# A one-core decoder step: modulation rows laid out whole, a zero fill and the decode work in other places

## The reference

```
mod = einsum('nd,de->ne', silu(c), ada_w) + ada_b          # 9 rows of 6 x 1024
sh1, sc1, g1, sh2, sc2, g2 = split(mod, 6)
h = rmsnorm(x, norm1_g) * (1 + sc1) + sh1
q, k, v, u = split(h @ w_in)                               # 8 heads of 64; u is 512 wide
att = dilated_attn_prompt(q, k, v, rel_bias)               # prompt rows: causal, three dilations
att = dilated_attn_decode(q, [cache_k, k], [cache_v, v])   # sample rows: over 2048 cached rows each
ssm_y, state = s5_branch(u, ...)                           # scan, GELU, then per-group GLU
mixed = concat(rmsnorm(att), rmsnorm(ssm_y))
x = x + g1 * (mixed @ w_out)
h2 = rmsnorm(x, norm2_g) * (1 + sc2) + sh2
x = x + g2 * hier_moe(h2)                                  # 16 experts, 2 of one group per token
y = rmsnorm(x, final_norm_g)
```

## Time and profile before

| | |
|---|---|
| runs | 800.74, 802.43, 807.8 us; median 802.43 |
| profiled execution | 809.11 us; span of its instructions 807.2 us |
| PE busy | 676.1 us (84%) |
| DVE, ACT, Pool busy | 291.5, 176.4, 126.4 us (36, 22, 16%) |
| mean granted clock of PE | 0.909 |
| DMA | 211.89 MB, mean 263 GB/s |
| chain that ended last | PE 69%, DMA 16%, SP's queue 5%, DVE 5%, ACT 3% |

### The profile page before, as it was taken

How to read it: one execution, slowest core, us unless ns; L and a number is a source line. 1 busy time by engine, 2 the same in 40 slices (tenths; PEclk the granted TensorE clock), 3 DMA queues, 4 the chain that set the end, 5 groups by cost and what they waited for, 6 DMA issues and landing times.

```text
span 807.2 us, 12020 instructions
## 1 busy us (share of the span) xinstructions
PE 676.1 (84%) x4885; PEld 392.6 (49%) x4885; DVE 291.5 (36%) x694; ACT 176.4 (22%) x362; POOL 126.4 (16%) x224
## 2 busy tenths in 40 slices
PE   3669999999999776899999499976899999999800
PEld 2558698888873343434456454422344444333200
DVE  4799665771111343325373641101110111110148
ACT  6010331222224365332121001100110100110033
POOL 2320006657500123110000000000000000000040
PEclk9879899999999988899987579999899999999955
DMA  8996147483784987997114929999999639999562
GB/s 285 386 265 231 58 160 270 161 283 112 226 183 152 365 323 180 364 344 254 59 59 177 319 65 388 395 391 409 396 399 374 234 105 364 396 401 400 218 238 110
DMA packets 93613, 211.89 MB, mean 263 GB/s; under 512 B 8716, under 2 KB 15404, under 8 KB 93269
## 3 DMA queue, kind: packets, MB, share of 16 engines
q1 hardware_dynamic: 82582, 182.49, 63.5%
q0 software_dynamic: 4976, 18.37, 7.3%
q10 hardware_dynamic: 6000, 10.25, 3.4%
HBM read 197.42 MB, written 18.91 MB: 268 GB/s over the span
## 4 chain that ended last, share of the span: by engine, by line
PE 69%; DMA 16%; SPq 5%; DVE 5%; ACT 3%; issue 2%; POOL 1%; ACTq 0%; POOLq 0%; DVEq 0%
PE ps L2555 18%; PE ps L2099 11%; PE ps L2597 9%; PE ps L2415 7%; DMA whalf<-in_w_down 5%; PE ps L2001 4%; DMA ring<-in_cache_v 4%; PE ps L2069 3%; PE ps L2007 2%; DMA ring<-in_ada_w 2%; SPq L510 2%; PE ps L2241 2%; PE ps L2216 1%; DMA whalf<-in_w_up 1%; SPq L660 1%
## 5 line engine op out<-in xcount | busy, mean ns | idle before, releaser
L2555 PE MATMUL ps<-whalf,xgT 128*128 128x512 f32 (+2 forms) x576 | 174.1, 612 | 9.1 <-DMA whalf<-in_w_up 5.2
L2555 PEld LDWEIGHTS ps<-whalf,xgT 128*128 128x128 f32 (+2 forms) x576 | 66.7, 158 | 107.8 <-issue 102.9
L2597 PE MATMUL ps<-whalf,aT 128*128 128x512 f32 (+2 forms) x288 | 87.8, 629 | 12.8 <-DMA whalf<-in_w_down 10.8
L2099 PE MATMUL ps<-hT,ring 128*128 128x272 f32 x384 | 91.4, 394 | 0.0
L2099 PEld LDWEIGHTS ps<-hT,ring 128*128 128x128 f32 x384 | 71.8, 190 | 15.2 <-issue 1.4
L2597 PEld LDWEIGHTS ps<-whalf,aT 128*128 128x128 f32 (+2 forms) x288 | 33.4, 160 | 60.3 <-issue 57.8
L2415 PE MATMUL ps<-ring,mixT 128*128 128x512 f32 x128 | 60.8, 634 | 1.9 <-ACT mixT L837 1.9
L807 POOL DMA_INDIRECT xg<-h_d,gidx x12 | 11.4, 948 | 226.4 <-PE ps L2001 185.3
L2415 PEld LDWEIGHTS ps<-ring,mixT 128*128 128x128 f32 x128 | 25.5, 203 | 32.7 <-issue 30.5
L1889 DVE COPY ysb<-ps 128x512 f32<-128x512 f32 x12 | 8.3, 691 | 91.6 <-PE ps L2597 91.6
L2069 PE MATMUL ps<-hT,ring 128*32 128x136 f32 x1024 | 36.8, 303 | 5.2 <-DVE hT L1373 4.0
(11 more groups left out here) (417 smaller groups left out, 921.0 us busy)
## 6 DMA issues: line engine op xcount, KB each, us to landing
whalf<-in_w_down SPq DMA_DIRECT2D x32, 1024.0 KB, 16.1
whalf<-in_w_gate SPq DMA_DIRECT2D x32, 1024.0 KB, 14.1
whalf<-in_w_up SPq DMA_DIRECT2D x32, 1024.0 KB, 14.3
ada_half<-in_ada_w SPq DMA_DIRECT2D x16, 1024.0 KB, 5.4
ring<-in_cache_k SPq DMA_DIRECT2D x8, 1792.0 KB, 7.7
ring<-in_cache_v SPq DMA_DIRECT2D x6, 2048.0 KB, 11.7
ring<-in_ada_w SPq DMA_DIRECT2D x4, 2048.0 KB, 14.7
ring<-in_w_in SPq DMA_DIRECT2D x4, 2048.0 KB, 13.4
```

What stands on the lines that cost most here:

```text
L2099: ins = mm(ps[:, z % 2, 0:2 * NCOL], r[:, 512 * k + P * (c % 4):512 * k + P * (c % 4 + 1)], hT[:, k, 2 * h:2 * h + 2, :].rearrange("p a b ...
L2555: ins = mm(out[cols, :], xgT[b][:, k, cols], r[:, 512 * (k % 4):512 * (k % 4 + 1)], start=k == 0, stop=k == KD - 1, **tile_at(m_, n))
L2597: ins = mm(ps[cols, 6 + n2, :], aT[:, t % 2, c, cols], r[:, c0:c0 + 512], start=c == 0, stop=c == 3, **tile_at(m_, n))
```

## The change

1. SP stores the modulation a second time, as nine whole rows of 4096 numbers (`mod_r`, nine DRAM-to-DRAM transfers after `kv(1)`). `mod2r`, `mod3P`, `mod3S` and `g2P` are read from there, so a piece is 12, 4 or 0.5 KB. `mod3P` is issued after `kv(12)` instead of `kv(9)`.
2. The zero fill of `y_d` goes from before the attention loop to behind the second store of `h2`, on the same Pool queue.
3. Pool clears `glu2` between two steps of the scan, and builds `qbd` before it fills `glu2`.
4. Group 0's keys stand between the V products, its softmax and transposes around the last one, group 1's keys between the bias tiles. `dPT` lies in another place of SBUF, and the new rows of V pass through another PSUM bank.
5. In the loop only group 1's transposes (round 1) and the values remain: group 0's in rounds 3 to 6, group 1's in rounds 8 to 11.

```diff
     def mod_rows(n, first):
-        return bass.AP(mod_d.tensor, 2 * first * P * P, [[0, P], [P * P, 2 * n], [32 * P, 4], [1, P]])
+        return bass.AP(mod_r.tensor, D * (first - 2), [[0, P], [1, D * n]])
...
             if i == 1:
...
-                for c in range(4):
-                    sp.dma_start(mod2r[4 * c:4 * c + 4, :],
-                                 bass.AP(mod_d.tensor, (6 + c) * P * P, [[32 * P, 4], [1, P]])).then_inc(s("cld"), 16)
-            if i == 9:
+                for r in range(NC):
+                    sp.dma_start(mod_r[r].rearrange("(c j n) -> c j n", j=4, n=P),
+                                 bass.AP(mod_d.tensor, P * (4 * P + r), [[P * P, 8], [32 * P, 4], [1, P]]))\
+                        .then_inc(s("cld"), 16)
+            if i == 3:
+                sp.wait_ge(s("cld"), 16 + 16 * NC)
+                sp.dma_start(mod2r[:, :], mod_r[0, D:3 * D].rearrange("(a n) -> a n", n=P)).then_inc(s("cld"), 16)
+            if i == 12:
                 sp.wait_ge(s("glut"), 16)
...
-                sp.dma_start(mod3P[:, :, :].rearrange("p v (c j n) -> p (v c) j n", c=2, j=4),
-                             mod_rows(3, 2)).then_inc(s("mod3"), 16)
+                sp.dma_start(mod3P[:, :, :].rearrange("p v n -> p (v n)"), mod_rows(3, 2)).then_inc(s("mod3"), 16)
...
         turn_back(4)
+        pool.wait_ge(s("xp"), len(BATCH))
+        o(pool.memset(glu2[:, :, :, :], 0.0))
         turn_back(5)
...
-        pool.dma_start(y_d[NREG * P:NTILE * P, :], I["zero"].partition_broadcast(EXTRA * P)).then_inc(s("yzero"), 16)
...
             pool.dma_start(h2_d[tok(j), :], h2[0:TW[j], p % 2, :]).then_inc(s_h2st[p % 2], 16)
+            if p == 1:
+                pool.dma_start(y_d[NREG * P:NTILE * P, :], I["zero"].partition_broadcast(EXTRA * P)).then_inc(s("yzero"), 16)
...
-        for n in range(16):
-            glu_out(n)
...
+        for n in range(10):
+            glu_out(n)
         dec_softmax(0)
+        dec_probs(0)
+        for n in range(10, 16):
+            glu_out(n)
+        dec_softmax(1)
...
         for n in range(3):
             glu_in(n)
+        dec_keys(0, 0)
         z_two(9)
...
             glu_in(n)
+        dec_keys(0, 2)
+        dec_keys(0, 3)
         z_two(11)
         v_t(2)
+        dec_probs_t(0)
         for n in range(10, 13):
             glu_in(n)
         v_t(3)
+        dec_keys(1, 0)
...
             if st == 1:
-                dec_probs_t(0)
-            if 2 <= st < 6:
-                dec_keys(1, st - 2)
-            if st == 6:
-                pe.wait_ge(s("cld"), 80)
+                dec_probs_t(1)
+                pe.wait_ge(s("cld"), 32 + 16 * NC)
                 tr(ps[:, 7, 0:16], mod2r[:, :]).then_inc(s("pe_prep"), 1)
-            if 9 <= st < 13:
-                if st == 9:
-                    pe.wait_ge(s("dve_prep"), M2E)
-                dec_values(0, st - 9)
-            if st == 13:
-                dec_probs_t(1)
-            if 14 <= st < 18:
-                dec_values(1, st - 14)
+            if st == 3:
+                pe.wait_ge(s("dve_prep"), M2E)
+            if 3 <= st < 7:
+                dec_values(0, st - 3)
+            if 8 <= st < 12:
+                dec_values(1, st - 8)
```

More of the change, by code:

```diff
@@ L203 @@
 GP, MODTP, DBP, M2P, ATTSP = range(1, 6)
-KMZ, PADT, BPAD, GLUB, QBD = range(1, 6)
+KMZ, PADT, BPAD, QBD, GLUB = range(1, 6)
 MODT, HMA, KME, SSRT = 1, 2, 3, 16
@@ L439, in mod_rows @@
     def mod_rows(n, first):
-        return bass.AP(mod_d.tensor, 2 * first * P * P, [[0, P], [P * P, 2 * n], [32 * P, 4], [1, P]])
+        return bass.AP(mod_r.tensor, D * (first - 2), [[0, P], [1, D * n]])
     def mod_rows_seq(n, first):
-        return bass.AP(mod_d.tensor, P + 2 * first * P * P, [[P, NSEQ], [P * P, 2 * n], [32 * P, 4], [1, P]])
+        return bass.AP(mod_r.tensor, D * (first + 2), [[4 * D, NSEQ], [1, D * n]])
     def ring_wait(eng, name):
@@ L621, in _ @@
         for t in range(TDEC):
-            sp.dma_start(mod3S[t:NS:TDEC, :, :].rearrange("p v (c j n) -> p (v c) j n", c=2, j=4),
-                         mod_rows_seq(3, 2)).then_inc(s("mod3s"), 16)
+            sp.dma_start(mod3S[t:NS:TDEC, :, :].rearrange("p v n -> p (v n)"), mod_rows_seq(3, 2)).then_inc(s("mod3s"), 16)
         sp.wait_ge(s("dOp"), 2)
@@ L764, in _ @@
         pool.dma_start(O["ssm_s"], xs[:, :, :, :].rearrange("p c s n -> p (c s n)")).then_inc(s("ssmst"), 16)
-        pool.wait_ge(s("xp"), len(BATCH))
-        o(pool.memset(glu2[:, :, :, :], 0.0))
+        o(pool.memset(qbd[:, :, :, :], 0.0))
+        pool.wait_ge(s("za"), 8)
+        for h in range(HEADS):
+            r = slice(64 * (h % 2), 64 * (h % 2) + 64)
+            o(pool.tensor_copy(qbd[r, :, h // 2, TDEC * h:TDEC * (h + 1)],
+                               qkT[r, h // 2, 0:NS].rearrange("p (n t) -> p n t", t=TDEC)))
+        pool.sem_inc(s("pool_prep"), 1)
         pool.wait_ge(s("glul"), 32)
@@ L1008, in bias_out, with dec_exp, dec_probs @@
             f(biasT[:, h, :], ps[:, (7, 4)[h % 2], :], ACT.Copy).then_inc(s("bfe"), 1)
+        def dec_exp(g):
+            act.wait_ge(s("dSm"), g + 1)
+            f(dP[:, :], dP[:, :], ACT.Exp, bias=dstat[:, 4:5], accum_out=dstat[:, 5:6]).then_inc(s("dP"), 1)
+        def dec_probs(g):
+            act.wait_ge(s("dPt"), g + 1)
+            if g:
+                act.wait_ge(s("dOp"), g)
+            f(dPT[:, 4:7, :], ps[:, 6, 0:3 * P].rearrange("p (a b) -> p a b", a=3), ACT.Copy)
+            f(dPT[0:NS, 7, :], ps[0:NS, 6, 3 * P:4 * P], ACT.Copy).then_inc(s("dPTe"), 1)
         z_two(8)
@@ L1025, in _ @@
         v_out(3)
-        f(vrow[0:NS, QT, :], ps[0:NS, 5, :], ACT.Copy).then_inc(s("ve"), 1)
+        f(vrow[0:NS, QT, :], ps[0:NS, 7, :], ACT.Copy).then_inc(s("ve"), 1)
         bias_out(0)
@@ L1162, in _ @@
         act.wait_ge(s("x2"), NT)
-        act.dma_start(g2P[:, :].rearrange("p (c j n) -> p c j n", c=2, j=4),
-                     mod_rows(1, 5)).then_inc(s("endld"), 16)
+        act.wait_ge(s("cld"), 32 + 16 * NC)
+        act.dma_start(g2P[:, :], mod_rows(1, 5)).then_inc(s("endld"), 16)
         for t in range(TDEC):
-            act.dma_start(mod3S[t:NS:TDEC, 0:1, :].rearrange("p v (c j n) -> p (v c) j n", c=2, j=4),
-                         mod_rows_seq(1, 5)).then_inc(s("endld"), 16)
+            act.dma_start(mod3S[t:NS:TDEC, 0, :], mod_rows_seq(1, 5)).then_inc(s("endld"), 16)
         act.dma_start(fgain[:, :], I["final_g"].partition_broadcast(P)).then_inc(s("endld"), 16)
@@ L2290, in _ @@
             glu_in(n)
+        dec_keys(0, 1)
         z_two(10)
```

43 lines of the change are left out of this document (13 added, 30 removed).

## The result

The changed kernel takes 802.0 us, the kernel before 810.76 in the same series of 20 runs each. The ratio is 0.9903, with a 95% interval of 0.9879 to 0.9928: some 8 us, 1.0%, where 11.2 us, 1.4%, were forecast (the two medians differ by 8.8 us). The 802.0 us lie above the range of 784.5 to 799.5. The sign was right and the time wrong, and the larger part of that is the base, the time of the kernel before from which the gain was taken off: the three runs shown (800.74, 802.43, 807.8) lay low for that kernel, whose medians in five series were 810.76, 811.1, 809.16, 806.7 and 810.17.

The account below looks back on a forecast made before the run. TensorE was 69% of the chain, DMA 16%, with a cached-value load held behind slow mod3P. Sum: -3.6 + 1.2 + 9.4 + 3.7 - 1.0 + 1.5 = 11.2 us, giving median 791.3; range 784.5 to 799.5.

Parts of the forecast that it names:

- In proportion the median 791.3: Whole kernel: 11.2 us off the profiled 809.11 gives 797.9, and in proportion the median of 802.43 becomes 791.3.
- S(11) to S(12): From the start of step 11's scores to step 12's: the cached-value wait goes, 4.5 us for 13.95, gain 9.4.
- The first rival: mod3P stays slow at its new place and the wait moves to step 9: 804.5 us; chance 0.06.
- Ahead of the loop: Before step 0's scores, S(0): moved decode work adds 8.6 us, waits and slow group save 5.0; S(0) 3.6 later.
- S(0) to S(11): Start of step 0's scores to step 11's, 42.9 us before: 1.2 gained, bounds -2.5 to 3.
- S(12) to the end: Start of step 12's scores to the loop's end: no decode work left, gain 3.7 us, bounds 2 to 5.5.
- the clock: Thinned last loop steps hold waits, so some matmuls may run at half clock: 1.0 us against, bounds 0 to 3.
- The decode moves together: Terms ahead of the loop, S(0) to S(11), S(12) to the end, and the clock: -3.6, +1.2, +3.7, -1.0 us.
- The gather: Gather after the loop: g2P's whole rows spare the queue just before it; gain 1.5 us, bounds 0 to 2.6.
- The fill behind the h2 stores: y_d's zero fill after the loop: 28.7 us, delays a store ACT waits for, 6 us of slack, cost nothing.
- DVE, ACT, Pool: Moved softmax, copies and Pool work: counted as nothing, bounds 0 to 1 us for DVE/ACT, -0.5 to 0.5 for Pool.
- the signs that were named for being right: No cached-load wait over 1 us; S(0) near 276.6, S(11) 318, loop end 343; mod3P within 10; gather 1 to 2 shorter.

Follow-up runs that it names:

- the two profiles after: Changed kernel profiled in its first series (802.0 us, 0.9903 of the kernel before) and once more, unaltered (802.1 us, 0.9908).
- the first two experiments: Kernel before with whole rows alone: 796.59 us, ratio 0.9846; changed kernel with mod3P read again in 512 B pieces: 813.82 us, ratio 1.0067.

## Why the prediction was wrong

*The base, the failing step.* "In proportion the median 791.3" took the gain off a median of three runs, although the profiled execution, at 809.11, had already shown a run above them all. The range counted nothing for the base. The base was 8.3 us too low, of the 10.7 us between 791.3 and 802.0. Against 810.76 the same sum gives 799.6, and the range moved with it, 792.8 to 807.8, would hold the 802.0. That the three runs lay low is chance, as far as is known. The 1.0% measured stands at the edge of the 1% that the prediction said a measurement can't tell; with 20 runs of each kernel the interval, 0.7 to 1.2%, clears zero.

The gain itself was also some 3 us too large. Up to the first output product the sum was 9.7 us; the two profiles after show 9.1 and 5.2 less than the one before. Term by term:

*S(11) to S(12)*: 9.4 forecast, 9.5 measured. That mod3P's transfer is what held the value load, and that whole rows shorten it, is shown by the first two experiments: undone it brings a wait of 11.5 us back, alone it gives all. 8.6 us were taken for it, by the rate of the zero fill; it took 12.0 to 12.4 in the changed order, 15 in the old one. Both arrive in time. The first rival, which needed some 17 us, is out.

*Ahead of the loop*: 3.6 later forecast. From z to S(0) it is 2.6 more (157.66 us before, 160.28 and 160.24 after). Keys 2 to 7 come in time because the fill has gone.

*S(0) to S(11)*: 1.2 forecast; 0.8 gained in one profile, 2.0 lost in the other, within the bounds of -2.5 to 3. The work is the same in both; the granted clock differs.

*S(12) to the end, and the clock*: the mis-sized term is the 1.0 us for the clock. 3.7 less 1.0 was forecast. To the first output product it was 25.42 us before (329.83 to 355.25), 23.98 and 25.19 after: 1.4 and 0.2 gained. With the waits filled it is 21.55 and 21.54, 3.9 gained. So the work was sized rightly, and the clock took 2.4 to 3.6 us here instead of 1.0; in one of the two profiles after, it took some 3 more in the rounds ahead.

*The decode moves together* (-3.6 + 1.2 + 3.7 - 1.0) were to give 0.3 us. Against whole rows alone they cost 5 ± 3, with the moves of the fill, of Pool's work and of mod3P counted in. The profiles show 2.2 to 3.9 us of it ahead of the loop, and from 2.3 gained to 1.9 lost in it; whether that is all, they don't show. The fill's move and the decode order hang together: with the fill left ahead of the loop the changed order takes 1.000 of the time before, with the fill moved 0.990, while in the old order the fill's move changes nothing that can be measured (0.9845 and 0.987). Pool's moves and mod3P's place were not tried one by one.

*The gather*: 1.5 forecast, 1.1 in the chain; from there to the end it is 343.3 us before, 344.1 and 342.0 after, so what is gained ahead does carry to the end. *The fill behind the h2 stores*: nothing forecast; it lands in 30.2 us, the stores take longer (a median of 5.5 us, 2.9 before), and ACT waits for none. *DVE, ACT, Pool*: nothing forecast; in the first profile after, one GLU product ahead of the loop waits 0.17 us for DVE, and in the loop group 1's first values wait 1.45 us for ACT's dPT copy.

Of the signs that were named for being right, most came: no wait for cached keys or values, S(0) at 275.95, S(11) at 318.04, a gather shorter by 1.1 us. mod3P's 12.0 us are over the 10 that were named, and the loop ended at 344.5 instead of 343.

The profile after is 12.5 us shorter than that of before, not 8: its execution was the fastest of the 20, which is luck. Of the 4.5 us, 2.7 stand in the last tile of the output projection (13.84 us on its chain, 16.53 before, 15.83 in the second profile after).

## What to carry to other kernels

Ask how many runs stand behind the base, and give a forecast as a gain against it; where the profiled execution lies above all of them, the base is part of the uncertainty. Work moved out of a loop that waits into a stretch in which the engine is never idle costs its full time there, and thins the loop: there the granted clock, not only the waits, has to be forecast. One layout that makes a slow transfer short can be the whole gain; try it alone first.

## What the runs showed of the hardware

The same 1.5 MB, one row into 128 partitions, took 27 to 31 us from issue to landing in pieces of 512 B that lie apart, and 11 to 15 us in rows of 12 KB, loads ahead of it in the queue included. An unaltered order of instructions ran its 70 us loop at a mean granted clock of 0.93 in one profile and 0.85 in another, and took 4 us more in the second; the falls to 0.50 stood behind waits of PE of 1.3 to 3.3 us, not at the same place each time. With products that nobody reads in some of those waits the loop ran at 1.00 in one profile; in another it ran at 0.95, where the clock fell in a round without them. From S(12) to the output projection, where they stood, both took 21.5 us for 24.0 to 25.2 without. The kernel of whole rows took 0.978 of the time before with such products in the later waits, 0.9845 without.
